# A norm and latent stage in another order: latent keys, values and queries ahead of the rotated rows, a table loaded one stage earlier, a fill of ones moved behind the maxima

## The reference, cut to what matters

```
aq = rms_norm(aq, a_q_norm); ak = rms_norm(ak, a_k_norm)       # 8 and 2 heads of 64
bq  = (rms_norm(bqd, b_q_norm) @ w_q_up)                        # 4 heads of 64 + 32
bkv = (rms_norm(bkvd, b_kv_norm) @ w_kv_up)                     # 4 heads of 64 keys + 64 values
# latent tokens only:
aq, ak = apply_rope(aq, rope_a), apply_rope(ak, rope_a)
bq_pe, bk_pe = apply_rope(bq_pe, rope_b), apply_rope(bk_pe, rope_b)
```

## Time and profile before

| what | us |
|---|---|
| median of 3 runs | 3808.43 (3808.2 to 3808.79) |
| the profiled execution, its own time | 3812.78 |
| its span in the profile | 3811.0 |
| TensorE busy in the span | 3415.3 (90%) |
| VectorE busy | 1986.4 (52%) |
| ScalarE busy | 1212.8 (32%) |
| norm and latent stage, layer 0, layer 1 | 525.5 to 666.6, 2497.7 to 2623.6 |
| attention up to the row of maxima, layer 0, layer 1 | 666.6 to 684.4, 2623.6 to 2641.3 |

### The profile page before, as it was taken

One profiled execution on the slowest core, in us unless ns is written; L12 is line 12 of the kernel. 1 busy time (PEld: TensorE's weight loads), 2 busy tenths in 40 slices (PEclk: granted clock), 3 DMA queues, 4 the chain that ended last, 5 costly groups with the idle time before them and its releaser, 6 DMA issues. The chain is left out here.

```text
span 3811.0 us, 45703 instructions
## 1 busy us (share of the span) xinstructions
PE 3415.3 (90%) x18969; PEld 1683.0 (44%) x18969; DVE 1986.4 (52%) x2923; ACT 1212.8 (32%) x1786; POOL 636.8 (17%) x372
## 2 busy tenths in 40 slices
PE   4999568899999999999997798577999899999997
PEld 2655432222245555555554555522322464444444
DVE  5682977566535333333336682967566363333334
ACT  3222643244434211111113222632344342222112
POOL 0000310478800000000000000301789100000000
PEclk8999879799999999999999899887999999999999
DMA  5210035100040111111101210051000301111111
GB/s 208 67 37 2 3 124 177 42 1 11 12 127 1 47 43 39 39 42 42 39 28 56 62 39 5 3 204 43 1 9 12 116 16 50 53 50 50 55 45 45
DMA packets 216735, 194.71 MB, mean 51 GB/s; under 512 B 10647, under 2 KB 180818, under 8 KB 216530
## 3 DMA queue, kind: packets, MB, share of 16 engines
q1 hardware_dynamic: 216530, 191.81, 16.0%
HBM read 168.00 MB, written 14.68 MB: 48 GB/s over the span
## 5 line engine op out<-in xcount | busy, mean ns | idle before, releaser
L705 PE MATMUL feed_acc<-feed_aa,feed_w 128*128 128x512 f16 (+1 forms) x3936 | 763.5, 355 | 0.0
L705 PE MATMUL feed_acc<-hh,feed_w 128*128 128x512 f16 (+1 forms) x3936 | 753.6, 354 | 5.2 <-DVE feed_w L987 5.2
L705 PEld LDWEIGHTS feed_acc<-feed_aa,feed_w 128*128 128x128 f16 x3936 | 388.8, 99 | 377.5 <-issue 15.3
L705 PEld LDWEIGHTS feed_acc<-hh,feed_w 128*128 128x128 f16 x3936 | 385.7, 98 | 370.2 <-DVE feed_w L987 5.8
L341 PE MATMUL in_acc<-hh,in_w 128*128 128x512 f16 (+1 forms) x2088 | 399.0, 354 | 75.5 <-DVE in_w L331 63.1
L1907 POOL TENSOR_TENSOR at_accp<-at_accp,at_p 128x1024 f32<-128x1024 f32 x192 | 451.5, 2352 | 84.3 <-ACT at_p L1940 76.4
L1961 DVE TENSOR_REDUCE at_mx<-at_small 128x1 f32<-128x512 f32 (+1 forms) x492 | 316.9, 686 | 246.3 <-PE at_small L2017 244.0
L1940 ACT ACTIVATE at_p<-at_sT 128x1024 f32<-128x1024 f32 x246 | 252.1, 1025 | 349.0 <-PE at_sT L2046 349.0
L341 PEld LDWEIGHTS in_acc<-hh,in_w 128*128 128x128 f16 (+1 forms) x2088 | 207.8, 100 | 264.5 <-DVE in_w L331 63.6
L1046 DVE SCALAR_TENSOR_TENSOR y<-feed_acc,y 128x1280 f32<-128x1280 f32 (+1 forms) x96 | 130.3, 1357 | 331.5 <-PE feed_acc L705 331.5
L1033 DVE TENSOR_TENSOR feed_r<-feed_r 128x1280 f32<-128x1280 f32 (+1 forms) x56 | 76.1, 1359 | 418.8 <-ACT feed_r L840 418.8
(11 more groups left out here) (295 smaller groups left out, 3962.0 us busy)
## 6 DMA issues: line engine op xcount, KB each, us to landing
pre<-in_w_ff SPq DMA_DIRECT2D x84, 512.0 KB, 4.0
pre_wada<-in_w_ada SPq DMA_DIRECT2D x20, 2048.0 KB, 7.9
feed_stage<-in_w_ff SPq DMA_DIRECT2D x44, 512.0 KB, 3.6
in_stage<-in_w_in SPq DMA_DIRECT2D x36, 512.0 KB, 4.6
set_wada<-in_w_ada SPq DMA_DIRECT2D x4, 2048.0 KB, 15.0
pre<-in_w_out SPq DMA_DIRECT2D x12, 512.0 KB, 5.1
x<-x_scratch SPq DMA_DIRECT2D x3, 2048.0 KB, 10.3
xin<-in_x SPq DMA_DIRECT2D x8, 512.0 KB, 7.1
```

The source lines that it names most:

```text
L705: last = nc.tensor.matmul(out[:, b:b + cn], w[:, wh, k, m0:m0 + P], src[:, sh, k, a + b:a + b + cn], start=(k == 0 and wh == 0 and sh == 0 ...
```

## The change

In `prepare`, the items `ak` and `aq0` to `aq3` of each chunk move behind the keys, values and queries; the places of squares, sums, mean, root, refinement and table turns stay. The table `sums` gets its memory in `mixers`, is loaded by SP in the readout `outputs`, which SP then waits for, and is no more loaded in `prepare`. ScalarE does the first `root` ahead of the first scaling of the cosine table. In `attention`, GpSimd fills the ones only after the first row of maxima is written, and TensorE waits for them no more at the start but before the first scores of a head pair below 4.

```diff
@@ mixers
                 input_projection(nc, e, sem, l, f)
+                f.sums, f.s_sums = sb("sums", [P, 8, 32], st=low, side="right"), sem(f"sums{l}_loaded")
                 recurrence(nc, e, sem, l, f)
@@ prepare
         names = ["ak"] + (["aq0", "aq1", "aq2", "aq3"] if query else [])
-        items += [("rope" if lat else "flat", x, c) for x in names]
         items += [("bk", h, c) for h in range(4)]
         items += [("bv", t, c) for t in range(a // P, (a + n) // P)]
         if query:
             items += [("bq" if lat else "bqraw", h, c) for h in range(4)]
+        items += [("rope" if lat else "flat", x, c) for x in names]
...
-        sums, cast = sb("sums", [P, 8, 32]), sb("cast", [P, 8, P])
+        sums, cast = f.sums, sb("cast", [P, 8, P])
...
-                sp.dma_start(sums[:, :, :], e.k_sums).then_inc(s_sel, 16)
                 sp.dma_start(cast[:, :, :], e.k_cast).then_inc(s_cast, 16)
...
                 for q in range(4, 8):
                     square(0, q)
+                root(0)
                 act.wait_ge(s_ca, 16)
                 nc.scalar.activation(cos["ak"], cos["aq"], ACT.Copy, scale=e.sv[:, l, R_AK:R_AK + 1]).then_inc(s_cos, 1)
-                root(0)
                 act.wait_ge(s_cos, 1)
...
-                pe.wait_ge(s_sel, 16)
+                pe.wait_ge(f.s_sums, 16)
                 four(0, 0)
@@ attention
+                pool.wait_ge(s_row, 1)
                 nc.gpsimd.memset(ks[64:65, :, :], 1.0).then_inc(s_ones, 1)
...
                             if pr < 4 and (pr, "q") not in loaded:
+                                pe.wait_ge(s_ones, 1)
                                 pe.wait_ge(s_load[pr % QRING], per_pair * (pr // QRING + 1))
...
                 ahead = ("max", "row")
-                pe.wait_ge(s_ones, 1)
                 tasks(-1, ahead)
@@ outputs
                 sp.dma_start(head_cast[:, :, :], e.k_head_cast).then_inc(s_con, 16)
+                sp.dma_start(f.sums[:, :, :], e.k_sums).then_inc(f.s_sums, 16)
+                sp.wait_ge(f.s_sums, 16)
```

More of the change, by code:

```diff
@@ L1299, in prepare @@
         bank = lambda i, role: W[slot[i, role] % 5]
-        (s_ca, s_cb, s_sel, s_upl, s_uh, s_ul, s_one, s_cos, s_sq, s_sum, s_m, s_r, s_n, s_p, s_first, s_rot, s_u,
+        (s_ca, s_cb, s_upl, s_uh, s_ul, s_one, s_cos, s_sq, s_sum, s_m, s_r, s_n, s_p, s_first, s_rot, s_u,
          s_hi, s_lo, s_kc) = (sem(nm + x) for x in (
-            "rope_a_loaded", "rope_b_loaded", "selectors_loaded", "up_loaded", "up_hi", "up_lo", "ones_set", "gains_in",
+            "rope_a_loaded", "rope_b_loaded", "up_loaded", "up_hi", "up_lo", "ones_set", "gains_in",
             "squared", "summed", "mean", "rsqrt", "newton", "products", "evacuated", "rotated", "u_ready",
```

## The result

| | before | after |
|---|---|---|
| median | 3808.61 us (3808.20 to 3812.85, 6 runs) | 3823.15 us (3821.37 to 3824.78, 6 runs) |
| profiled execution | 3812.78, span 3811.0 | 3823.56, span 3821.8 |

The ratio is 1.0035, 95% interval 1.0023 to 1.0048: slower by more than 0.2%. The forecast of 3815.4 had this time in its range (3806 to 3824), but its likeliest case, within 0.2%, did not happen.

A forecast was written before the change was run, and what follows sets the result against it. TensorE was busy 90% of the span, but in the norm and latent stage TensorE and VectorE alternate as the limit. Stages +8.3, clock falls +3.2, attention -4.5 make +7.0: 3819.8 us profiled, median 3815.4, range 3806 to 3824.

The forecast's parts named there:

- The order of the queues: Norm and latent stage: queue work in the new order, clock high, adds 2.7 us in layer 0, 5.6 in layer 1: +8.3.
- Chunk 0: First rotated row's start to chunk 1's shared key rotation: 48.2 us in layer 0, +1.1 there and +2.7 in layer 1.
- Chunk 1: From its shared key rotation to the context chunk's first scaling: 51.2 us in layer 0 (-1.2), 49.0 in layer 1 (+1.8).
- Context chunk: Last chunk of the stage: 15.2 us against 12.4 in layer 0 (+2.8), and +1.1 in layer 1.
- VectorE idles some 2.5: Chunk 0: VectorE waits some 2.5 of the 4.05 us of other TensorE work ahead of the last query's rotation.
- the term of the clock falls: Stage: TensorE drops toward 1.2 GHz once per layer on the path, 1.6 us each from the nearest row: +3.2.
- the first rival: TensorE's clock falls twice per layer in dense stretches: 3.2 to 7 us more, 3818.6 to 3824; 0.44 together with another rival.
- The second rival: Rotated rows fill half of VectorE's idle time in the stage's dense stretches: 24 us less, 3787; 3 in 100.
- The loads: Early table of sums, issued in the readout: worth 0, bound 0.3 us per layer.
- the third rival: Clock stays high everywhere, also earlier at attention's start: 3809, no difference; 0.50 together with the forecast's own case.
- Attention: Start of attention: the moved fill shortens VectorE's cast of the identity, 2.25 us less per layer, -4.5; lower bound 0.6.
- the same difference: Last step: the new median lies 4.35 us below the profiled execution, as the old did, so 3819.8 becomes 3815.4.

The follow-up runs named there:

- e_gap: Changed kernel plus 128x128 products that nobody reads, put in TensorE's gaps ahead of keys and in refinements: 3820.60 us, ratio 1.0026 to the old kernel.
- e_rot_first: Changed kernel with the last query's rotation ahead of the first rotated row, the second four sums behind that row's products: 3813.35 us, ratio 1.0003 to the old kernel.
- r_after: Changed kernel run once more, unaltered, for a second trace: 3823.18 us, ratio 1.0032 to the old kernel.
- e_fill: Old kernel with only GpSimd's fill of ones moved behind the first row of maxima: 3807.24 us, ratio 0.9990 to the old kernel.
- r_before: Old kernel run once more, unaltered, for a second trace: 3812.29 us, ratio 1.0003.
- e_load: Old kernel with only the table of sums loaded in the readout and the first root ahead of the cosines: 3808.43 us, ratio 0.9994 to the old kernel.
- e_order: Old kernel with only the new order of the items (rotated rows behind keys, values and queries): 3824.68 us, ratio 1.0032 to the old kernel.
- e_twice: Changed kernel with the first (permuting) product of each rotated row issued twice: 3825.76 us, ratio 1.0042 to the old kernel.
- e_warm: e_old_order with the twenty score products of the first attention unit issued twice: 3809.47 us, ratio 0.9999 to the old kernel.
- e_old_order: Changed kernel with the items back in the old order, late fill and early load kept: 3804.82 us, ratio 0.9983 to the old kernel.
- e_turns: Changed kernel with five of layer 1's eight table turns moved back among rotated and scaled rows: 3818.07 us, ratio 1.0018 to the old kernel.

## Why the prediction came out as it did

**The order of the queues was right.** With the clock held up, the forecast lengths can be read in `e_gap`, which does not depend on the forecast. Chunk 0: 48.2 forecast for layer 0, 48.17 measured; for layer 1, 45.5 + 2.7 = 48.2 forecast, 48.16 measured. Chunk 1: 51.2 forecast and 51.40, 49.0 forecast and 49.39. Context chunk of layer 1: +1.1 forecast, +0.96. That of layer 0 took 17.34 and not 15.2, since its turn was at the low clock there too (3.62 instead of 1.9), which leaves 15.6. Two of the forecast's sums were added up too low, as redoing them shows: TensorE's queue in chunk 1 of layer 1 is 22.1 and not 21.8, so 49.3, and the context chunk's terms in layer 0 make 15.6. With them the stages' +8.3 would have been +9.0. The step "VectorE idles some 2.5" measured 2.12, and `e_rot_first` showed it to be worth 2.2 per chunk 0.

**The step that failed is the term of the clock falls**: "I take one per layer on the path at 1.6", +3.2. Against `e_gap` the changed kernel lost 1.45 and 1.56 in the two chunks 0 and 2.05 in chunk 1 of layer 1. In the context chunk of layer 0 its turn and first three key products took 3.78 instead of 2.41 at the high level, 1.37 more. That is 6.4 in all: four falls, not two. Their mean of 1.6 is the nearest row's 1.6; the price was right and the count wrong. The forecast had named the gap in each refinement and the thin stretch ahead of each block of keys, then counted one of them per layer. That the fall in layer 0's refinement costs nothing shows in `r_after`, whose chunk 0 had that fall and not the one at the first keys and took 48.16. `e_gap` shows the cause for those of chunks 0 and 1; for the context chunk of layer 0 it is read from the trace alone, and the falls don't come in the same places each time (`r_after`). This is the mechanism of the first rival, which "decides from 0.6 us above my sum on", and the falls beyond the forecast alone were 3.2. Its own bounds were uneven: two falls per layer at 2.9 add 8.4 and not 7 to the sum, as its 3824 has it. The second rival's 3787 is likewise 24 us off the old span and not off the forecast, from which it would be 3791.

**Two effects were not in the sum, and nearly cancel in the profiled runs.** The loads were taken at 0 with a bound of 0.3 per layer; up to the low halves they gave 2.4 in layer 0 and 0.4 in layer 1 against the first trace of the old kernel, and 1.8 in layer 1 against its second. TensorE was at a higher clock in the second four sums (3.06 against 4.80 in layer 0, 3.90 and 4.80 in the two traces of layer 1), which is 1.7 of the 2.4. The forecast looked for the first four sums, which indeed ended where they did, and not for what an earlier start of TensorE does to its clock. Against that, the start of attention in layer 1 ran 18.8 us at the low clock instead of 8.4, and attention lasted 3.6 longer; the third rival had considered the opposite. What made the rise late is not known, so these 3.6 us are measured and not explained.

**Attention: right.** 2.3 per layer of the forecast 2.25, by the mechanism named (`e_fill`). By the Trainium skill, page "SBUF — State Buffer", section "Who interferes with whom", a copy or cast of VectorE in a two-port mode and an instruction of GpSimd lock each other out of a shared port pair for a whole instruction. The cast (2.27 us beside the fill, 0.23 without it) agrees. So does the copy of line 93, which ends at 529.9 in the old trace with GpSimd's fill of 4.36 us from 525.55; no run took that fill away.

**From profile to median.** The sum was +7.0 and the profiled runs differ by 10.8. The other 4 us of the miss come from the step "the median before is 3808.43, 4.35 below it; the same difference": the old kernel's profiled run is among the longest of its executions (3808.2 to 3812.85 here), while the changed kernel's (3823.56) lies 0.4 from its median. The spread differs between the two kernels, and the distance can't be carried from one to the other.

The account in us of span: the order without falls +8.8 (forecast +8.3), falls +6.4 (+3.2), loads -2.8 (0), maxima -4.6 (-4.5), rest of attention +3.0 (0). That is +10.8 against +7.0. The +8.8 is what is left of the stages' +12.4 when falls and loads are taken out. Layer 1's part of it hangs on which trace of the old kernel is taken, since its chunk 1 took 47.22 in one and 44.81 in the other.

**Where it was luck.** The range held the time, but its upper end was made of two falls per layer at 2.9. The falls were two per layer at 1.6; what brought the time near the end of the range was the 4 us from profile to median, for which the forecast had no bound, while loads and attention happened to cancel.

What stays open: why the clock at the start of layer 1's attention rises 8 us behind the first scores in some kernels (before, `r_before`, `e_load`, `e_rot_first`), after 13 in others (`e_order`, `e_twice`, `e_warm`), and after 18 to 20 in the rest (after, `r_after`, `e_fill`, `e_old_order`, `e_gap`, `e_turns`). It repeated in the two kernels that were traced twice, and in layer 0 it came earlier with more work on TensorE before it (`e_warm`), but also with the fill moved alone (`e_fill`, 8.3 us instead of 19.8); what decides it was not found. Nor was it tested that steps of some 4 us in the old kernel's spread are one such late rise, though the sizes agree.

## What to carry to other kernels

Before moving work between a stretch bound by TensorE and one bound by another engine, list every TensorE gap in the new order and what stands behind it: here the work right behind the gaps of 2.4, 3.7 and 5.1 us ran in whole or part at 1.2 GHz (in one trace the work behind 2.4 us did not), and that costs time where this work opens a TensorE-bound stretch. Small independent work (table turns) is worth most inside those gaps, and least right behind one. Split a change of several parts: here two of the three were a gain of 0.17% that the third hid, and the version without the third is the one to keep.

## What the runs showed that I had not expected

- The granted clock at the start of attention, with TensorE 94% busy (16.92 of 18 us), stayed at 1.2 GHz for 18 to 24 us in some traces and about 8 in others, and one late rise was worth 3.6 to 4.4 us (attention of 329.5 against 325.9 in layer 1, 357.4 against 353.0 in layer 0).
- A fall of the clock did not come every time behind the same gap: behind 2.37 us ahead of the first keys, nine products took 3.59 in one trace of the changed kernel and 2.13 in the other.
- Starting TensorE 1.1 us earlier shortened the second four sums by 1.7 us (4.80 to 3.06, layer 0), though the squares they need came only 0.1 us earlier.
- GpSimd's fill of one partition row made a 128x128 cast ten times as long (0.23 to 2.27 us), and a 128x16 copy beside another such fill took 3712 ns, where one of the same size in the setup took 176.
- Not every fall costs time. Of ten stretches at 1.2 GHz in the changed kernel's two stages four made them longer. The old kernel's own falls in chunk 1 of layer 1 came in one trace (47.22 us) and not in the other (44.81).
